# A hybrid decoder layer: the copies of the sliding-window state issued by ScalarE instead of GpSimd, with rows of 2 KB as packets

## What is computed

```python
h = x + concat(latent_attention, dilated_window_attention) @ w_out
g = rmsnorm(h) @ w_gate                     # 1088 x 1024 @ 1024 x 2816
u = rmsnorm(h) @ w_up
gc = conv_b + sum(conv_w[j] * gp[:, j:j + T] for j in range(3))   # causal, depthwise
y = rmsnorm(h + (silu(gc) * u) @ w_down)
# and, for each of the 8 sequences, the window state moved on by 8 tokens:
s_win_k = concat([state_win_k[:, 8:], new_k], axis=1)   # 8 x 2048 rows x 512 floats (2 KB a row)
s_win_v = concat([state_win_v[:, 8:], new_v], axis=1)
```

## Time and profile before

| | |
|---|---|
| time, median of 3 runs | 1790.83 us (1786.58 to 1793.28) |
| the profiled execution | 1785.58 us, of which the span is 1783.4 us |
| PE busy | 1701.5 us (95% of the span) |
| PEld, DVE, ACT, POOL busy | 1485.6, 863.5, 661.8, 578.4 us |
| MLP, from the first up product to the last down product | about 985 to 1748 us of the span |
| one iteration of the MLP | 71.8 us |
| state copies | 20 DMAs of 3264 KB |

### The profile page before, as it was taken

The page is one execution under the profiler, slowest core; times in us unless marked ns, Lnnn a source line. Parts: engine busy times, 40 slices in busy tenths (PEclk is TensorE's granted clock), DMA queues, the critical chain, the costliest instruction groups (busy, mean ns, idle before and its releaser), DMA issues.

```text
span 1783.4 us, 27781 instructions
## 1 busy us (share of the span) xinstructions
PE 1701.5 (95%) x9857; PEld 1485.6 (83%) x9857; DVE 863.5 (48%) x1828; ACT 661.8 (37%) x1331; POOL 578.4 (32%) x531
## 2 busy tenths in 40 slices
PE   7999979999997999999899999999999999999996
PEld 6788868888886888888788989888888898888885
DVE  6433335677675776767434332433433324334235
ACT  5222135667675666665322312212112121121113
POOL 0000004566561867778301312212213122121121
PEclk9999977999998999999999999999999999999998
DMA  8232243233306565755612668586595875865912
GB/s 286 101 106 91 97 125 103 70 79 97 80 15 169 166 180 159 186 161 162 224 49 51 137 140 134 132 170 110 117 166 120 155 127 130 163 122 119 154 43 105
DMA packets 156062, 227.46 MB, mean 128 GB/s; under 512 B 31063, under 2 KB 128984, under 8 KB 149528
## 3 DMA queue, kind: packets, MB, share of 16 engines
q1 hardware_dynamic: 153086, 159.39, 30.2%
q0 software_dynamic: 2880, 66.85, 23.0%
HBM read 201.12 MB, written 91.93 MB: 164 GB/s over the span
## 4 chain that ended last, share of the span: by engine, by line
PE 48%; DMA 1%; DVE 1%; ACT 1%; POOL 0%; issue 0%; SPq 0%; ACTq 0%; DVEq 0%; POOLq 0%
PE wide L2646 22%; PE turn L2668 14%; PE rest L2647 7%; PE wide L2321 4%; DMA o_work<-scratch_s_o 1%; PE wide L2744 1%; DMA out_y_prompt<-f_gc 0%; DMA acc<-in_w_gate 0%; PE turn L2333 0%; ACT f_gc L2551 0%; DVE f_gc L2615 0%; PE rest L2653 0%; DVE acc L2570 0%; POOL f_gl L2723 0%; ACT f_rows L2558 0%; POOL f_st L2479 0%
## 5 line engine op out<-in xcount | busy, mean ns | idle before, releaser
L2668 PE MATMUL turn<-lead,f_ah 128*128 128x512 f32 x792 | 240.6, 394 | 5.4 <-DVE f_al L2603 4.0
L2570 DVE TENSOR_TENSOR acc<-turn,acc 128x512 f32<-128x512 f32 x198 | 136.6, 691 | 189.8 <-PE turn L2668 189.8
L2646 PE MATMUL wide<-hT_h,lead 128*128 128x512 f32 x704 | 184.9, 354 | 0.0
L2668 PEld LDWEIGHTS turn<-lead,f_ah 128*128 128x128 f32 x792 | 147.9, 189 | 39.9 <-DVE acc L2570 5.9
L2441 POOL TENSOR_TENSOR f_gl<-f_graw,f_gh 128x1024 fp32r<-128x1024 f32 x21 | 50.6, 2409 | 364.2 <-ACT f_gh L2486 364.2
L1099 POOL TENSOR_SCALAR a_pr<-a_pr,a_rden 128x256 f32<-128x256 f32 (+7 forms) x128 | 94.0, 746 | 188.8 <-DVE a_rden L1199 184.1
L2584 DVE SCALAR_TENSOR_TENSOR f_gc<-wide,f_coef,f_gc 128x832 f32<-128x832 f32 x44 | 47.7, 1085 | 208.0 <-ACT f_lasts L2506 205.1
L2668 PE MATMUL turn<-lead,f_al 128*128 128x512 f32 x352 | 137.2, 390 | 0.0
L804 PE MATMUL zp<-win_h,xT_h 128*128 128x512 f32 (+1 forms) x288 | 112.8, 392 | 3.3 <-DVE acc L655 3.3
L804 PE MATMUL zp<-win_l,xT_h 128*128 128x512 f32 (+1 forms) x288 | 111.3, 387 | 0.0
L2646 PEld LDWEIGHTS wide<-hT_h,lead 128*128 128x128 f32 x704 | 107.6, 188 | 0.0
(11 more groups left out here) (368 smaller groups left out, 4417.1 us busy)
## 6 DMA issues: line engine op xcount, KB each, us to landing
out_s_win_k<-in_state_win_k POOLq DMA_DIRECT2D x10, 3264.0 KB, 43.2
out_s_win_v<-in_state_win_v POOLq DMA_DIRECT2D x10, 3264.0 KB, 45.7
acc<-in_state_win_k SPq DMA_DIRECT2D x16, 768.0 KB, 6.2
acc<-in_state_win_v SPq DMA_DIRECT2D x16, 768.0 KB, 5.7
f_uraw<-in_w_up SPq DMA_DIRECT2D x22, 512.0 KB, 4.6
f_draw<-in_w_down SPq DMA_DIRECT2D x11, 1024.0 KB, 34.1
f_graw<-in_w_gate SPq DMA_DIRECT2D x21, 512.0 KB, 8.2
acc<-in_cache_kv_latent SPq DMA_DIRECT2D x128, 64.0 KB, 1.8
```

Of the source, the lines that this page charges most:

```text
L2570: nc.vector.tensor_tensor(a, dp[h][:], a, ALU.add).then_inc(S["d_add"], 1)
L2646: nc.tensor.matmul(out[:, c0:c1], w[n][:, k, :], x[:, k, c0:c1], start=s, stop=e)
L2668: last = nc.tensor.matmul(dp[h][:], a[:, c, t * P:(t + 1) * P], w[:, c, h * 512:(h + 1) * 512], start=(c == 0 and j == 0), stop=(c == 1 an ...
```

## The change

The copies leave GpSimd's stream and enter ScalarE's: at the start of each `body(i)` ahead of `chunk(i, 0)`, and for i = 0 in `first`, behind the copy of the coefficients and ahead of `chunk(0, 0)`. Each of the two copies of an iteration becomes two, one of the even rows and one of the odd rows of the 204, so that runs on either side are single rows of 2 KB. An iteration issues four DMAs of 8 sequences by 102 rows where it issued two of 8 by 204. The bytes are the same.

```diff
+CHUNK = (PAST - DEC_T) // MOVES
...
+def move(eng, io, first, rows):
+
+    for src, dst in (("state_win_k", "s_win_k"), ("state_win_v", "s_win_v")):
+        a = io[src][:, bass.ds(first + DEC_T, rows), :].rearrange("b (r s) c -> s b r c", s=2)
+        b = io[dst][:, bass.ds(first, rows), :].rearrange("b (r s) c -> s b r c", s=2)
+        for s in range(2):
+            eng.dma_start(b[s], a[s]).then_inc(io["moved"], 16)
...
@@ gpsimd
-            def move(i):
-                n = (PAST - DEC_T) // MOVES
-                for src, dst in (("state_win_k", "s_win_k"), ("state_win_v", "s_win_v")):
-                    pool.dma_start(io[dst][:, bass.ds(i * n, n), :], io[src][:, bass.ds(i * n + DEC_T, n), :])\
-                        .then_inc(io["moved"], 16)
-
             def body(i):
                 split("g", i * 2 + 1)
                 split("u", i * 2 + 1)
                 split_d(i)
-                move(i)
...
@@ scalar, first(i)
                 act.wait_ge(S["coef"], 1)
+                move(act, io, 0, CHUNK)
                 chunk(0, 0, True, False)
                 chunk(0, 1, True, False)
 
             def body(i):
+                move(act, io, i * CHUNK, CHUNK)
                 chunk(i, 0, True, True)
                 chunk(i, 1, True, False)
...
-"moves": 16 * 2 * MOVES
+"moves": 16 * 4 * MOVES
```

More of the change, by code:

```diff
@@ L2832, in hybrid_decoder_step @@
     with ExitStack() as ctx:
-        io = {**io, "ident_sb": ctx.enter_context(nc.sbuf_tensor("ident_sb", [P, P], F32)), "moved": ctx.enter_context(nc.semaphore("moved")), "moves": 16 * 2 * MOVES}
+        io = {**io, "ident_sb": ctx.enter_context(nc.sbuf_tensor("ident_sb", [P, P], F32)), "moved": ctx.enter_context(nc.semaphore("moved")), "moves": 16 * 4 * MOVES}
         sems = io["sems"] = Semaphores(nc)
```

## The result

The changed kernel takes 1999.16 us (median of 4 runs, 1993.29 to 2006.37) against 1789.53 us: a ratio of 1.117, 95% interval 1.113 to 1.122. 1978 us were forecast. The profiled execution has a span of 2004.6 us.

The account below looks back on a forecast made before the run. TensorE was taken as the bound in the MLP. Pauses of 17.3 us in nine iterations (156 us), 19 us in iteration 0 and 16 us of clock made 191 us on 1785.6, given as 1978 us, range 1788 to 2110.

Parts of the forecast that it names:

- The bound and the slack: MLP stretch: TensorE is busy throughout; ScalarE's issues may take 16.85 us before TensorE waits for down-product additions.
- ScalarE is held: Ahead of chunk 2i's eviction: four DMA issues keep ScalarE 34.2 us, so TensorE waits 17.3 us an iteration.
- Eight engines: The copies of 8 x 102 rows: outermost dimension 8 puts each on 8 DMA engines, 102 packets on each.
- Why it is held: ScalarE's queue: 128 to 144 outstanding packets per engine fit, so 268 to 284 of 412 must be through first.
- The copies' time: One iteration's copies on eight engines: 45 us, with memory staying the limit, between bounds of 36 and 88 us.
- The sum: Whole kernel: 156 us over nine iterations, 19 in iteration 0, 16 for clock; 191 us on 1785.6, given as 1978.
- clock: TensorE after each of ten pauses: the granted clock falls for a while, 1.6 us each, 16 us together.
- The gate loads: Gate weights loaded beside the copies: ScalarE's 19.65 us wait goes away, worth nothing because it lies under the down product.
- The late bound: Rival at ScalarE's issues: copies run on 16 engines, issue phase 17 to 20 us, 1805 us; chance 0.13 including its other form.
- a bound on the queue's sum: Rival at ScalarE's queue: room is 2048 to 2304 packets over all engines, 1805 us; shares the late bound's 0.13.
- a queue that holds nothing: Rival at ScalarE's queue: all four issues taken at 0.37 to 0.6 us each, time stays at 1786 us; chance 0.11.
- the slow pace: Rival on the copies: eight engines keep the slow pace, 88 us, issue phase 63 us, 2265 us in all; chance 0.06.

Follow-up runs that it names:

- two and two: The change's four DMAs on ScalarE, keys' pair at the start of chunk 2i, values' pair at chunk 2i+1: 1802.09 us, ratio 1.0067 to the kernel before.
- large packets: ScalarE issues the copies at the change's place but unsplit, two DMAs of 8 x 204 rows an iteration: 1801.46 us, ratio 1.0065 to the kernel before.
- on sixteen engines: ScalarE at the change's place, 2 KB packets, one DMA each for keys and values, 192 rows outermost: 1791.39 us, ratio 1.0001 to the kernel before.
- the run with 184: As with 192 rows outermost, but 184 rows, leaving eight engines with 184 packets each per DMA: 1794.37 us, ratio 1.0015 to the kernel before.
- The quarters: The change's copies cut in four instead of two, eight DMAs of 8 x 51 rows an iteration, same place: 2001.25 us, one execution.

## Why the prediction was right

Point by point:

- *The bound and the slack.* Right. The 16.85 us of the earlier trace rows fit: a hold of 36.8 us (1241.2 to 1278.0) gave a pause of 19.86 us, one of 19.22 us in "two and two" 1.98 us, and holds of up to 14.4 us none. I had left out two things that nearly cancel: TensorE can still fill the second PSUM bank, about 1 us, and the addition that it then waits for takes 0.69 us itself.
- *ScalarE is held.* Right, and not by its queue or its place as such, as the runs with large packets and on sixteen engines show.
- *Eight engines.* Right: 8 completions to a DMA. The rule of the Trainium skill cited in the prediction ("DMA: Bandwidth & Descriptors", section "Why a DMA increments its semaphore by 16 and not by 1") held here, and for 192 rows and 184 rows as outermost dimension as well (16 and 8).
- *Why it is held.* Wrong in kind, near in size. I took the earlier trace rows for a room of 128 to 144 per engine that a DMA's own packets must fit in. The change's second DMA went through on top of 102 at once, 204 together, and the run with 184 showed that what lies ahead counts, some 75 to 100 per engine at the end of most holds, and not the sum with its own. For the last of four DMAs of equal size the two readings differ less than they might: 268 to 284 of 412 must be through by mine, 412 - 103 - 81 = 228 by the trace. The earlier trace rows itself, recounted, does not give one figure either: the down load began with 128 packets per engine ahead on SyncE's queue and was let through with about 50.
- *The copies' time.* Too short: 45 us taken, some 58 us measured (first packet to last, beside the weight loads). This term and the one before it were both wrong and pulled in opposite directions, so that their product came out well: 34.2 us of hold forecast, 34.9 measured as the mean of ten. That closeness is luck. I had also taken 45 us because the memory would be the limit; no run shows that it is, and the same bytes went through in 38 us in large packets. The window of one iteration (1240 to 1301) has the pace:

```profile
q10 hardware_dynamic: 3296, 6.68, 40.9%
```

0.409 x 16 x 61 / 3296 = 0.121 us a packet, 17 GB/s per engine. Eight engines do better otherwise: with large packets 6.68 MB took about 38 us, and with 184 rows outermost 6.03 MB some 39 us. So eight engines and 2 KB packets, even together (184 rows), do not make the change's copies slow. What the change has beside them is that a DMA takes every other row and, if the outermost dimension is dealt out to the engines, one sequence on each; which of these it is was not tried apart. The quarters, with every fourth row, took 43 to 53 us. The figure of the Trainium skill for rows 4 MiB apart (103 GB/s; "DMA: Bandwidth & Descriptors", section "Latency and other measured facts") comes near to the change's 6.68 MB in 58 us, 115 GB/s, but the large packets, with the same distance between the sequences, ran at 176.
- *The sum.* Forecast 17.3 us of pause, measured 18.6; clock 1.6 us each, measured some 2.3; iteration 0, 19 us, measured 21.1. Total 191 forecast on 1785.6; measured 210 by the medians. Every term is a little low, and the period came out at 92.7 us where I had written 87 to 91. The 210 are not all this chain: some 10 us of the profiled execution lie ahead of the MLP.
- *The gate loads.* The 19.65 us waits of the earlier trace rows are gone, as forecast, and were worth nothing. SyncE's down load went from 28.09 us in the earlier trace rows to 0.74 to 1.78 us, worth nothing either.
- *Rivals.* The late bound (1805 us) fell with the eight engines, and its other form, a bound on the queue's sum, with the run on sixteen (3072 packets taken at once); the one of a queue that holds nothing fell with the 35.01 us; the slow pace (2265 us) overstated: 58 us and not 88; and the run without copies shows that there was nothing to win.

## What to carry to other kernels

A DMA on an engine's queue is an instruction of that engine, and on ScalarE's queue it stood here while more than some 100 packets of 2 KB per DMA engine lay ahead of it. Cost it by that hold less the slack at its place: some 31 us of hold cost nothing under the down product, 35 us ahead of the eviction cost 21 us an iteration. So before moving DMAs onto a compute engine count packets per engine and the number of DMAs: rows of 2 KB instead of large runs multiply the packets, and an outermost dimension of 8 halves the engines. Either of two things was enough here: sixteen engines by an outermost dimension that 16 divides (192 rows; 184 rows left eight engines), or two larger DMAs instead of four. And ask first what the move could win: a wait of 20 us that nobody on the critical path sees is worth nothing.

## What the runs showed of the hardware that I had not expected

- On ScalarE's queue with packets of 2 KB an issue waits for the number of packets ahead, not for the sum with its own: 184 per engine went through on top of 84. Most held issues ended with 74 to 101 per engine left, two of every eight quarters with 103 to 122.
- That figure is not one of every queue. In the run with large packets SyncE's gate load at 1053.69 was held for 15.96 us with 609 packets ahead in all, and let through with 545. In this time its 64 packets of 512 bytes went through beside 56 large ones and 8 completions of the copies. If what lay ahead was on the eight engines of the copies, it was 76 and 68 on each, an estimate. What sets the figure is open. ScalarE's queue (q10) and SyncE's (q1) from 1053.7 to 1069.6:

```profile
q10 hardware_dynamic: 64, 2.92, 48.7%
q1 hardware_dynamic: 64, 0.03, 0.7%
```

- GpSimd's queue holds in another way: issues of some 0.96 us with up to about 130 packets per engine ahead (16 engines, by the completions), but one in nine waited until the queue was empty, up to 28.07 us.
- Neither the size of the packets nor the number of engines sets the pace of a copy within HBM by itself, beside weight loads: rows of 2 KB on sixteen engines moved 6.29 MB in about 37 us (170 GB/s), packets of 52 KB on eight engines 6.68 MB in 38 us (176), the same packets on GpSimd's queue in the kernel before took some 45 us (148), and the change's 58 us (115).
